# Two-layer block on one core: order of the heads, of the prologue and of the norms between layers changed

## The chip, the cores and the metric

One Trainium2 chip, one of its cores. The kernel is one launch on that core. The metric is the device time of an execution in microseconds (us); three executions of the kernel before stand below. Engines are named as the profile names them: PE is TensorE, DVE VectorE, ACT ScalarE, POOL GpSimd, SP SyncE.

## The reference

A sequence of 512 tokens with 1024 features (and a context of 256 tokens) goes through a block of two layers and then through one hybrid layer. What matters here:

```python
# layer 0 (even mixer)
hx = modulate(rmsnorm(x, g0), shift, scale)      # shift, scale, gate = silu(c) @ mod_w[0] + mod_b[0]
hc = modulate(rmsnorm(ctx, g0), shift_c, scale_c)
# 8 heads of 128 features, first over the context (for the state), then over x
u  = depthwise_conv(xb, sconv_w, sconv_b)        # 4 taps
r, i = sigmoid(u @ w_r + b_r), sigmoid(u @ w_i + b_i)
a  = exp(-8 * r * softplus(-lam));  bx = sqrt(1 - a*a) * i * u
h[t] = a[t] * h[t-1] + bx[t]                     # one scan forward, one backward
y_b = (h_forward + h_backward) * silu(gb)
y_a = silu(layernorm(conv31(va * sigmoid(vg)))) * silu(ga)
x = x + gate * (concat(y_a, y_b) @ w_out)
# layer 1 (odd mixer)
x = x + gate1 * pooled_mixer(modulate(rmsnorm(x, g1), shift1, scale1))
x = rmsnorm(x, final_g)
# hybrid layer: h = rmsnorm(x, norm1_g), four branches, merge, feed-forward, last rmsnorm
```

The output is (1, 512, 1024) in float32.

## The kernel before

Activations lie with features on the 128 partitions and tokens along the row: a tile is 128 features by 512 tokens (256 for the context), and X, h_hi, h_lo have 8 of them. A float32 product is made of three passes: weights and activations are each split into a high and a low part (float32r), and `three` multiplies high by high, high by low and low by high. `blocks` does this for up to 8 blocks of 128 features; a whole product of 24 matmuls of 512 columns is one "chunk" of weights.

Weights come in 284 chunks of 512 KB in the order of `NAMES`. Each goes through a ring of four slots: SP issues its DMA (L382), ACT makes the high part (`hi`, L412), DVE the low part (`lo`, L843), each three chunks ahead of the product (`ahead`). PE waits for the low part (`ready`). All engines run a fixed program in order; the order of the work of an engine is the order of the code in `act()`, `dve()`, `pe()`, and semaphores tie them.

**Prologue.** ACT issues the DMAs of the modulation weights (`mod0`, four of 2 MB), of X (2 MB) and of the context (1 MB). PE forms the modulation rows (`mod_rows`, L1466, two columns of weights and 128 moving columns at a time) and turns them into columns (`mod_columns`, L1472). ACT squares the tiles of X, DVE adds the squares up (L884), one matmul with ones sums over the features and spreads the sum over all partitions (`feature_sum`, L1459), ACT takes the root and DVE the reciprocal (L888). Then `norm_low` and `norm_high` (L912, L434, L919) make the 8 tiles of the context and then the 8 of X. After the last of them POOL issues the DMA of c for the other modulation columns (`csb`, L393), and ACT waits for it before the first head (L476).

**Heads.** First eight heads over the context (products xc, vg, va, gc), then eight over x (xb, gb, ga, gx, and the convolution cw of 31 taps, 128x32 tiles of the array, L1541). In each, ACT copies xb into `xp` (L485), DVE does the four taps (L977, L980), ACT and DVE split u (L489, L852), PE multiplies by the gates (gc or gx), ACT evaluates the gates (`head_gates`, L499 to L506), DVE forms the drive (`head_drive`, L990, L991), ACT takes two roots (`head_roots`, L511), DVE scans (`head_scan`, L997 to L1005), and in the heads over x adds, multiplies and splits the result (L1048, L1051, L552, L852). All of one head is done before ACT and DVE go on to the next one's xb. DVE also does 32 reductions of 128x1024 (`conditioning`, L904), two in each head, whose operand POOL loads two ahead (`MOD_RING`).

**After the heads.** PE sums csum, DVE subtracts the mean from the 8 tiles of U (mu, L1065, L1069), ACT squares them, DVE adds, PE sums, and meanwhile PE does the products yb 0 to 2, then yb 3 to 7 and ya 0 to 7. **Between layers** (after ya, and after od) DVE adds the product to X, ACT squares, DVE adds the squares, PE sums over features (128x512), ACT takes the root and DVE the reciprocal of 128x512; then norm tile by tile, and the first product (u 0, or qk 0) takes the tiles as they come. Between layer 1 and the hybrid layer there are two such sums, and X is scaled by the second afterwards.

Of the kernel before, what the change touches and what calls it, by code (L numbers as in the profile page):

```python
# [13 lines left out]
AHEAD = 3  # L14
KC = 8
# [23 lines left out]
def vector_columns():  # L39
    at, cols = 0, {}  # L40
    for name, n in (
# [5 lines left out]
        ("ssm_d", 2), ("ssm_norm_g", 2), ("norm2_g", NT), ("final_g2", NT), ("w_dt", NT * NH),  # L47
# [48 lines left out]
def bank_uses():  # L96
# [27 lines left out]
    "vec x ctx cst cst2 out hi lo mm crep csb mdv v a zero eps pad sil sp_z sp_e wdt rows cols rows_c x_sum x_sq fsum f_sq "  # L124
    "norm_t norm_hi norm_lo xp conv uhi ulo gread e2 mv sq thr scan sig uu "
    "tgt sgb sgat sga cpe csum yact ybhi yblo ymu usum usq yln ysil yga yhi yalo res xsq xsum "
    "lpad lcp dhi dsub dlo gsil gy gyhi gylo ores osq osum hsum "
    "bk4 bk5 bk6 bk7 ya_hi ya_lo yb_hi yb_lo yc_hi yc_lo yd_hi yd_lo ctap cact dtm dts dte dta "
    "st_qk st_abs st_ln st_sp st_in st_zb st_w st_wp st_pv mo_qk mo_mx mo_p mo_n mo_pt mo_cp mo_pv "
    "ma_cs ma_xt ma_xd ma_gm ma_gc ma_tri ma_abc ma_row ma_d ma_e ma_dk ma_pv ma_yt ma_sq ma_y mp mt mhi mlo "  # L130
    "wres wg whi wsq wsum wlo fg fsil fup fr fhi flo fres fsq fss fin"
# [40 lines left out]
def program(nc, wts, modw, modt, crep, vecs, consts, x_in, ctx_in, out):  # L172
# [66 lines left out]
    yb_hi = p("yb_hi", NT * T, F32R)  # L239
    yb_lo = p("yb_lo", NT * T, F32R)  # L240
    mraw = p("mraw", MOD_RING * CW)
# [16 lines left out]
    sq, rstd0, rstd_c, ssum = (aa[0], aa[1]), th[0], th[1], tg  # L258
# [4 lines left out]
    csil = small[:, 0:2 * NT]  # L263
# [12 lines left out]
    cs3 = csil.rearrange("p (k two) -> p k two", two=2)  # L276
    mv0 = modv0.rearrange("p (k two) -> p k two", two=2)
# [4 lines left out]
    rstd_b = at("rstd_b", T, limit // 32 * 32 - 2 * K * 5)  # L282

# [9 lines left out]
    rstd1, n_t1 = lev0[0][:, 0:T], [lev[:, T * k:T * (k + 1)] for k in range(3)]  # L293
# [26 lines left out]
    rstd2, r2, n_t2 = zs[:, 0:T], zs[:, T:2 * T], [bc[:, T * k:T * (k + 1)] for k in range(3)]  # L320
# [37 lines left out]

    def sp():
# [13 lines left out]
        e.wait_ge(s_mod0[1], 16)  # L373
        for c in range(N_CHUNKS):
# [13 lines left out]
    def pool():  # L388
# [9 lines left out]
        e.wait_ge(S["osum"], 2 * (NT - 1))  # L398
        e.dma_start(cst2[:, :], consts[:, 512:NCONST]).then_inc(S["cst2"], 16)

    def act():
# [25 lines left out]

        def norm_high(q, w, hi_t, shift, tmps):
# [8 lines left out]
        for j in range(4):  # L437
            e.dma_start(mod0[:, j * 4 * CW:(j + 1) * 4 * CW].rearrange("p (a n) -> p a n", a=4),
                        modw[4 * j:4 * j + 4, :, :].rearrange("a p n -> p a n")).then_inc(s_mod0[j], 16)
            if j == 0:  # L440
                e.dma_start(X[:, :], x_in).then_inc(S["x"], 16)
            if j == 1:
                e.dma_start(ctx_x[:, :], ctx_in).then_inc(S["ctx"], 16)
# [9 lines left out]
        e.wait_ge(S["x"], 16)  # L453
        for k in range(NT):
            if k > 2:
                e.wait_ge(S["x_sum"], k - 2)
            fn(ssum[:, :] if k == 0 else sq[k % 2][:, :], tile(X, k), ACT.Square).then_inc(S["x_sq"], 1)
        e.wait_ge(S["eps"], 1)
        root(1, rstd0, 0, eps_rms, D)
        e.wait_ge(S["ctx"], 16)  # L460
        for k in range(NT):
            e.wait_ge(S["x_sum"], NT - 1 + max(k - 2, 0))
            fn(ssum[:, 0:TC] if k == 0 else sq[k % 2][:, 0:TC], tile(ctx_x, k, TC), ACT.Square).then_inc(S["x_sq"], 1)
        for j in range(2):
            e.wait_ge(S["rows"], j + 1)
            fn(rows0[0:2, j * T:(j + 1) * T], bank(2 + j)[0:2, :], ACT.Copy).then_inc(S["rows_c"], 1)
        root(2, rstd_c[:, 0:TC], 1, eps_rms, D, TC)
        for c in range(AHEAD):
            hi(c)
        for j in range(2, 4):  # L470
            e.wait_ge(S["rows"], j + 1)
            fn(rows0[0:2, j * T:(j + 1) * T], bank(2 + j)[0:2, :], ACT.Copy).then_inc(S["rows_c"], 1)
# [18 lines left out]
        def head_gates(I, w, gates):  # L491
            if I:
                e.wait_ge(S["scan"], I)
# [38 lines left out]
        for i in range(NT):  # L532
# [3 lines left out]
            if i:  # L536
                convolved(i - 1)
# [1431 lines left out]
```

## Time and profile before

| | |
|---|---|
| three executions | 1792.26 us median, 1791.04 to 1792.68 |
| the profiled execution's own time | 1792.62 us |
| its span, first to last instruction | 1791.3 us |
| mean granted TensorE clock | 0.970 |
| PE busy | 1673.2 us, 93% |
| DVE busy | 992.5 us, 55% |
| ACT busy | 746.1 us, 42% |
| POOL busy | 19.4 us |

The span leaves 1.3 us of the execution's time outside. Busy PE counts a matmul from its start to its modelled end; matmuls overlap, so one of 512 columns is some 0.39 us long while the next begins 0.23 us after it. The rest of the profile is read as waits: in a timeline row the bracket says how long the engine was idle before this row and what released it.

### The profile page before, as it was taken

To read this page: it belongs to the slowest core of one execution; us is meant where nothing else is said; L and a number is where in the kernel's file an instruction comes from. 1 tells how busy PE (TensorE), PEld (TensorE's weight loads), DVE (VectorE), ACT (ScalarE), POOL (GpSimd) and SP (SyncE) were. 2 spreads that over 40 slices of the span, in tenths; PEclk is the share of its full clock that TensorE was granted. 3 is DMA by queue.
4 is the path that set the end of the run, shared out by engine and by line. 5 is a ranking of instruction groups with operands and counts; after the bars stand their busy time and mean duration, and the time that the engine had idled before them with its cause. 6 is when DMAs were issued, how large, how long until landed. Compare 5 with 4: busy or idle time off the path is not lost.

```text
span 1791.3 us, 19102 instructions
## 1 busy us (share of the span) xinstructions
PE 1673.2 (93%) x7670; PEld 1297.0 (72%) x7670; DVE 992.5 (55%) x1362; ACT 746.1 (42%) x1014; POOL 19.4 (1%) x40
## 2 busy tenths in 40 slices
PE   6798899996997999999799989999999999999996
PEld 4677666664785888888587857776677788888885
DVE  4677768777757556744744453345545544444333
ACT  3567665765434333332334444334433322332221
POOL 0000000000000000000000000000000000000000
PEclk9799999998998999999899989999999999999998
DMA  7345536454231233232132111221122233232321
GB/s 315 117 159 182 190 129 202 150 178 154 71 106 59 94 97 104 91 100 94 46 111 69 67 47 55 77 70 56 62 94 95 83 102 98 95 94 94 106 94 47
DMA packets 55063, 190.46 MB, mean 106 GB/s; under 512 B 7328, under 2 KB 7328, under 8 KB 54720
## 3 DMA queue, kind: packets, MB, share of 16 engines
q1 hardware_dynamic: 47616, 159.52, 27.4%
q0 software_dynamic: 4960, 18.20, 3.1%
q10 hardware_dynamic: 2400, 11.53, 1.6%
q8 instruction: 61, 1.00, 0.2%
q14 instruction: 26, 0.21, 0.0%
HBM read 178.63 MB, written 2.10 MB: 101 GB/s over the span
## 4 chain that ended last, share of the span: by engine, by line
PE 71%; DVE 14%; ACT 10%; issue 4%; ACTq 1%; DMA 0%; DVEq 0%
PE banks L1446 21%; PE banks L1448 21%; PE banks L1447 21%; ACT w_hi L412 2%; PE banks L1693 2%; DVE w_lo L843 2%; DVE u L980 2%; PE banks L1466 1%; ACT aa L504 1%; ACT tr L506 1%; DVE ti L997 1%; DVE tr L1001 1%; DVE tr L1005 1%; ACT tr L499 1%; PE banks L1715 1%
## 5 line engine op out<-in xcount | busy, mean ns | idle before, releaser
L1446 PE MATMUL banks<-h_hi,w_hi 128*128 128x512 f32 x1408 | 561.1, 398 | 24.4 <-DVE h_lo L919 10.3
L1447 PE MATMUL banks<-h_lo,w_hi 128*128 128x512 f32 x1408 | 553.1, 393 | 0.0
L1448 PE MATMUL banks<-h_hi,w_lo 128*128 128x512 f32 x1408 | 552.3, 392 | 0.0
L843 DVE TENSOR_TENSOR w_lo<-raw,w_hi 128x1024 fp32r<-128x1024 f32 x276 | 336.5, 1223 | 295.5 <-ACT w_hi L412 295.1
L412 ACT ACTIVATE w_hi<-raw 128x1024 fp32r<-128x1024 f32 x276 | 288.2, 1050 | 159.2 <-PE banks L1448 147.8
L1446 PEld LDWEIGHTS banks<-h_hi,w_hi 128*128 128x128 f32 x1408 | 266.7, 189 | 102.6 <-issue 34.4
L1448 PEld LDWEIGHTS banks<-h_hi,w_lo 128*128 128x128 f32 x1408 | 267.3, 190 | 56.9
L1447 PEld LDWEIGHTS banks<-h_lo,w_hi 128*128 128x128 f32 x1408 | 267.5, 190 | 53.8 <-issue 0.7
L1446 PE MATMUL banks<-y_hi,w_hi 128*128 128x512 f32 x192 | 76.8, 400 | 5.7 <-ACT gs L716 5.6
L1448 PE MATMUL banks<-y_hi,w_lo 128*128 128x512 f32 x192 | 76.8, 400 | 0.0
L1447 PE MATMUL banks<-y_lo,w_hi 128*128 128x512 f32 x192 | 76.1, 396 | 0.0
L1448 PE MATMUL banks<-f_hi,w_lo 128*128 128x512 f32 x176 | 70.2, 399 | 0.0
L1447 PE MATMUL banks<-f_lo,w_hi 128*128 128x512 f32 x176 | 69.4, 394 | 0.0
L1446 PE MATMUL banks<-f_hi,w_hi 128*128 128x512 f32 x176 | 69.0, 392 | 0.0
L716 ACT ACTIVATE gs<-banks 128x512 f32<-128x512 f32 x32 | 19.1, 598 | 110.9 <-PE banks L1448 110.8
L1541 PE MATMUL banks<-rep,raw 128*32 128x512 f32 x512 | 56.8, 594 | 0.0
L1446 PEld LDWEIGHTS banks<-y_hi,w_hi 128*128 128x128 f32 x192 | 36.4, 190 | 16.7 <-issue 4.4
L1414 DVE TENSOR_TENSOR fs<-banks,fs 128x512 f32<-128x512 f32 x22 | 15.2, 692 | 55.7 <-PE banks L1448 55.7
L1466 PE MATMUL banks<-mod,small 128*2 128x128 f32 x256 | 32.5, 295 | 13.9 <-ACT small L447 13.9
L1124 DVE TENSOR_TENSOR lev<-lev 128x632 f32<-128x632 f32 (+3 forms) x40 | 31.6, 791 | 24.5 <-ACT lev L598 23.5
L823 ACT ACTIVATE f_hi<-fs 128x512 fp32r<-128x512 f32 x22 | 13.9, 633 | 73.0 <-DVE fs L1416 73.0
L1447 PEld LDWEIGHTS banks<-y_lo,w_hi 128*128 128x128 f32 x192 | 36.4, 190 | 8.9
(347 smaller groups left out, 2145.8 us busy)
## 6 DMA issues: line engine op xcount, KB each, us to landing
raw<-weights SPq DMA_DIRECT2D x284, 512.0 KB, 3.5
mraw<-modt POOLq DMA_DIRECT2D x32, 512.0 KB, 4.5
mod<-modw ACTq DMA_DIRECT2D x4, 2048.0 KB, 23.0
rep<-U SPq DMA_DIRECT2D x96, 64.9 KB, 2.7
rep<-U SPq DMA_DIRECT2D x32, 64.8 KB, 2.5
X<-x_in ACTq DMA_DIRECT2D x1, 2048.0 KB, 13.2
out<-X SPq DMA_DIRECT2D x4, 512.0 KB, 2.7
ctx_x<-ctx_in ACTq DMA_DIRECT2D x1, 1024.0 KB, 19.8
```

Of the source, the lines that this page charges most:

```text
L412: fn(slot(w_hi, c), slot(raw, c), ACT.Copy).then_inc(S["hi"], 1)
L499: own.did(fn(tr[k][:, 0:w], gates[2 * k], ACT.Tanh, bias=at_c(144), scale=0.5))
L716: fn(gs[j][:, :], bank(4 + j), ACT.Sigmoid).then_inc(free("mg", br, half, j), 1)
L843: tt(slot(w_lo, c), slot(raw, c), slot(w_hi, c).bitcast(F32), ALU.subtract).then_inc(S["lo"], 1)
L980: m = stt(u[:, 0:w], xp[:, k:k + w], sw(k), u[:, 0:w], ALU.mult, ALU.add)
L1124: own.did(tt(here[:, :, wn // 2:wn // 2 + n], below[:, :, shift0:shift0 + n], below[:, :, shift0 + wn // 2:shift0 + wn // 2 + n], ALU.add))
L1446: mm(o, wh, r_hi, start=start, stop=False)
L1447: mm(o, wh, r_lo, start=False, stop=False)
L1448: return mm(o, wl, r_hi, start=False, stop=stop)
L1466: last = mm(bank(2 + j)[0:2, t * P:(t + 1) * P], csil[:, 2 * k:2 * k + 2], w, start=k == 0, stop=k == KC - 1)
L1541: last = mm(banks[32 * j:32 * j + 32, 3 * 512:4 * 512], slot(raw, c, (8 * j + step) * 32, 32), rep[i % 2][:, a:a + T], start=step == 0, st ...
L1693: last = mm(banks[p0:p0 + HD, OUT * 512 + n * P:(OUT + 1) * 512], v[:, n * 256 + h * HD:n * 256 + (h + 1) * HD], blk(w, n), start=n == 0, ...
```

## The change

Six things are changed.

1. Prologue: ACT issues X in two halves, the context, then the modulation weights in another layout (128 rows of 16 KB each) in the order of groups 0, 2, 1, 3, with the first three chunks of weights between the second and third group. `mod_rows` takes 32 stationary columns and 512 moving ones in four column groups of the array; `mod_columns` is a product with `pick`. The squares are summed by eight matmuls with ones instead of DVE adds. The norm's tiles come in two halves of the features: context 0 to 3, x 0 to 3, then context 4 to 7, x 4 to 7, and the first products (xc, vg, va of head 0) likewise, with `mod_rows(3)` and `mod_columns(2)`, `(3)` among them.
2. Heads as a pipeline of two: the roots, the drive, the scans and the result of head i-1 are done during head i. `conditioning` is done once in a head over the context and three times in a head over x. In heads over x the result lies in tr[0] instead of u; one of the tensors th has eight buffers.
3. After the heads, the first seven eighths of yb 0, 1, 2 come before the last head's result is needed; csum is summed after the first of them.
4. Norm between layers by columns of tokens: `token_sum` multiplies the squares (stationary, 128x128) by a column, so that sums lie with tokens on partitions (128x4); root and reciprocal are of 128x4; `token_scales` makes four diagonal blocks and `spread` multiplies ones by them, and the norm reads the result from PSUM. The sum of the first seven tiles is begun inside the last product.
5. The first two products after each of these norms go together, tile by tile.
6. The three memsets before the pooling are moved from DVE to POOL; X is scaled by the final norm behind products qk 0 to 2, and PE waits for that (`xfin`) ahead of the attention.

```diff
@@ sp, pool
-        e.wait_ge(s_mod0[1], 16)
-        for c in range(N_CHUNKS):
+        e.wait_ge(s_mod0[2], 16)
+        for c in range(AHEAD, N_CHUNKS):
...
+        e.wait_ge(S["norm_lo"], 3 * NT)
+        for t in (lev0[0], lev0[1], lev):
+            e.memset(t[:, :], 0.0).then_inc(S["lpad"], 1)
@@ act
-        for j in range(4):
-            e.dma_start(mod0[:, j * 4 * CW:(j + 1) * 4 * CW].rearrange("p (a n) -> p a n", a=4),
-                        modw[4 * j:4 * j + 4, :, :].rearrange("a p n -> p a n")).then_inc(s_mod0[j], 16)
...
+        for j in range(2):
+            e.dma_start(X[:, j * 4 * T:(j + 1) * 4 * T], x_in[:, j * 4 * T:(j + 1) * 4 * T]).then_inc(S["x1" if j else "x"], 16)
+        e.dma_start(ctx_x[:, :], ctx_in).then_inc(S["ctx"], 16)
+        for j, g in enumerate(GROUPS):
+            if j == 2:
+                for c in range(AHEAD):
+                    e.dma_start(slot(raw, c), wts[c, :, :]).then_inc(s_raw[c], 16)
+            e.dma_start(mod0[:, j * 4 * CW:(j + 1) * 4 * CW], modr[g, :, :]).then_inc(s_mod0[j], 16)
...
+        rows_copy(0)
+        rows_copy(1)
         for c in range(AHEAD):
             hi(c)
+        for n in range(4):
+            first_high(n)
+        rows_copy(2)
+        for n in range(4, 7):
+            first_high(n)
+        rows_copy(3)
+        first_high(7)
...
@@ act, heads over the context and over x
             head_input(i, TC, 4)
+            head_high(i, TC)
             ahead("vg", i)
+            if i:
+                head_roots(i - 1)
...
-            head_roots(i, TC)
...
             ahead("xb", i)
+            if i:
+                convolved(i - 1)
+            head_roots(NT + i - 1)
             product("xb", i)
             head_input(NT + i, T, 0)
             if i:
-                convolved(i - 1)
+                head_high_out(i - 1)
+            head_high(NT + i, T)
...
-            head_roots(NT + i, T)
-            e.wait_ge(S["yact"], i + 1)
-            fn(tile(yb_hi, i), u[:, :], ACT.Copy).then_inc(S["ybhi"], 1)
         convolved(NT - 1)
+        head_roots(2 * NT - 1)
+        head_high_out(NT - 1)
@@ dve, heads over the context
             ahead("xc", i)
-            head_input(i, TC)
+            if i:
+                head_drive(i - 1, TC)
+            head_conv(i, TC)
             ahead("vg", i)
+            head_low(i, TC)
+            if i:
+                context_scan(i - 1)
             ahead("va", i)
+            conditioning(i)
...
@@ dve, heads over x
             ahead("xb", i)
-            head_input(NT + i, T)
+            head_drive(NT + i - 1, T if i else TC)
             if i:
                 convolved(i - 1)
+                head_sum(i - 1)
+            else:
+                context_scan(NT - 1)
+            head_conv(NT + i, T)
+            if i:
+                head_low_out(i - 1)
             ahead("gb", i)
+            head_low(NT + i, T)
+            conditioning(NT + 3 * i)
...
@@ dve, between layers
-        inverse(4, rstd1)
-        norm_low(2, X, T, rstd1, lambda k: g1[:, k:k + 1], lambda k: modv1[:, k:k + 1], h_hi, h_lo, n_t1)
+        token_scales(4, 0)
+        e.wait_ge(S["rb"], 1)
+        norm_low(2, X, T, bank(6), lambda k: g1[:, k:k + 1], lambda k: modv1[:, k:k + 1], h_hi, h_lo, n_t1)
+        def token_scales(n, o):
+            e.wait_ge(S["f_sq"], n)
+            own.did(e.reciprocal(rc[:, o:o + NB], rc[:, o:o + NB]))
+            own.wait()
+            for j in range(NB):
+                ts(dg[:, j * P:(j + 1) * P], ident, rc[:, o + j:o + j + 1], None, ALU.mult).then_inc(S["dg"], 1)
@@ pe
+        def token_sum(b, total, w, start, stop):
+            n = w.shape[1]
+            for j in range(NB):
+                last = mm(bank(b, n, n * j), total[:, j * P:(j + 1) * P], w,
+                          start=start and j == 0, stop=stop and j == NB - 1)
+            return last
+        def spread(b, n):
+            for j in range(NB):
+                e.wait_ge(S["dg"], NB * n + j + 1)
+                last = mm(bank(b, P, j * P), ones, dg[:, j * P:(j + 1) * P], start=True, stop=True)
+            last.then_inc(S["rb"], 1)
         def mod_rows(j):
             e.wait_ge(s_mod0[j], 16)
-            for t in range(4):
-                for k in range(KC):
-                    w = mod0[:, (4 * j + t) * CW + k * P:(4 * j + t) * CW + (k + 1) * P]
-                    last = mm(bank(2 + j)[0:2, t * P:(t + 1) * P], csil[:, 2 * k:2 * k + 2], w, start=k == 0, stop=k == KC - 1)
+            for k in range(KC):
+                q = k % 4
+                last = mm(bank(ROWS_BANK[j])[32 * q:32 * q + 32, :], cs[:, 32 * k:32 * k + 32],
+                          mod0[:, j * 4 * CW + k * T:j * 4 * CW + (k + 1) * T], start=k < 4, stop=k > 3)
...
         for f in range(3):
-            yb(f)
+            yb_early(f)
+            if f == 0:
+                e.wait_ge(S["csum"], NT)
+                feature_sum(0, csum[:, :])
+        for f in range(3):
+            yb_late(f)
         e.wait_ge(S["usum"], NT - 1)
         feature_sum(1, ti[0][:, :])
...
+                blocks(bank(BANK_OF[f]), c, h_hi, h_lo, n=5, start=False, stop=False)
+                e.wait_ge(S["xsum"], NT - 2)
+                token_sum(7, s1[:, :], s_one, True, False)
+                blocks(bank(BANK_OF[f]), c, h_hi, h_lo, b0=5, k0=5, n=3, start=False).then_inc(S["mm"], 1)
...
+            if g == 0:
+                c0, c1 = ready("u", 0, 0), ready("u", 0, 1)
+                for k in range(KC):
+                    e.wait_ge(S["norm_lo"], 2 * NT + k + 1)
+                    m0 = three(bank(0), c0, k, tile(h_hi, k), tile(h_lo, k), k == 0, k == KC - 1)
+                    m1 = three(bank(1), c1, k, tile(h_hi, k), tile(h_lo, k), k == 0, k == KC - 1)
```

## Rows read from the trace of the kernel before

**Rows 1.** The page's first part: busy time, share of span, instructions of each engine.

```profile
PE 1673.2 (93%) x7670; PEld 1297.0 (72%) x7670; DVE 992.5 (55%) x1362; ACT 746.1 (42%) x1014; POOL 19.4 (1%) x40
```

**Rows 2.** Timeline of the prologue: start, length, engine, line, operation; idle before and releaser.

```profile
3.02 9.14 ACTq L438 DMA_DIRECT2D mod<-modw  x2
...
41.81 8.81 PE L1466 MATMUL banks<-mod,small 128*2 128x128 f32 x64
...
52.32 0.88 DVE L912 SCALAR_TENSOR_TENSOR n_t<-ctx_x,small,th 128x256 f32<-128x256 f32 x2
...
68.81 1.63 DVE L919 SCALAR_TENSOR_TENSOR h_lo<-n_t,small,h_hi 128x512 fp32r<-128x512 f32 x2
...
74.74 1.06 ACT L476 ACTIVATE csb<-csb 128x1024 f32<-128x1024 f32 x1 [3.78 <-DMA csb<-crep]
```

**Rows 3.** Windows: length, busy time of each engine, PE clock, DMA share, GB/s.

```profile
20.00:36.00 16.00, 16.00 (x141) 11.78 (x139) 6.59 (x7) 6.04 (x10) 0.00 (x0) 1.00 1.02 408
```

**Rows 4.** Timeline of ACT and DVE in one head over the context.

```profile
121.54 0.47 ACT L499 ACTIVATE tr<-banks,small 128x256 f32<-128x256 f32 x1
...
126.06 0.42 DVE L990 SCALAR_TENSOR_TENSOR th<-tr,th 128x256 f32<-128x256 f32 x1 [1.44 <-ACT tr L506]
...
127.98 1.05 ACT L412 ACTIVATE w_hi<-raw 128x1024 fp32r<-128x1024 f32 x1
...
131.46 1.21 DVE L843 TENSOR_TENSOR w_lo<-raw,w_hi 128x1024 fp32r<-128x1024 f32 x1
...
134.59 0.42 ACT L489 ACTIVATE u_hi<-u 128x256 fp32r<-128x256 f32 x1 [5.30 <-DVE u L980]
...
139.66 0.46 ACT L499 ACTIVATE tr<-banks,small 128x256 f32<-128x256 f32 x1
```

**Rows 5.** Timeline of ACT, DVE and PE in one head over x.

```profile
400.52 0.69 ACT L499 ACTIVATE tr<-banks,small 128x512 f32<-128x512 f32 x1
...
410.68 0.69 DVE L997 TENSOR_TENSOR ti<-ti,xp 128x512 f32<-128x512 f32 x1
...
416.36 0.63 ACT L552 ACTIVATE yb_hi<-u 128x512 fp32r<-128x512 f32 x1 [5.78 <-DVE u L1051]
...
418.56 0.47 PE L1446 MATMUL banks<-h_hi,w_hi 128*128 128x512 f32 x1 [0.81 <-ACT xp L485]
...
422.85 0.63 ACT L489 ACTIVATE u_hi<-u 128x512 fp32r<-128x512 f32 x1 [4.43 <-DVE u L980]
...
427.27 7.09 PE L1541 MATMUL banks<-rep,raw 128*32 128x512 f32 x64
...
428.24 0.69 ACT L499 ACTIVATE tr<-banks,small 128x512 f32<-128x512 f32 x1
```

**Rows 6.** All uses of the modulation columns' operand: time from issue to landing.

```profile
DMA to landing us min/median/max: 3.7/4.5/7.8
```

**Rows 7.** Timeline of PE and DVE after the last head.

```profile
447.22 2.08 PE L1459 MATMUL banks<-csum,cst 128*128 128x512 f32 x2 [12.87 <-DVE csum L1029]
...
449.34 0.69 DVE L1065 TENSOR_SCALAR aa<-banks 128x512 f32<-128x512 f32 x1 [1.80 <-PE banks L1459]
...
468.04 1.12 PE L1459 MATMUL banks<-ti,cst 128*128 128x512 f32 x2 [0.49 <-DVE ti L1076]
```

**Rows 8.** Windows after that idle time, columns as in rows 3.

```profile
448.00:452.00 4.00, 4.00 (x9) 2.68 (x8) 1.98 (x3) 1.21 (x3) 0.00 (x0) 0.50 0.00 0
```

**Rows 9.** Timeline between layers 0 and 1.

```profile
540.88 0.75 DVE L1094 SCALAR_TENSOR_TENSOR X<-banks,small,X 128x512 f32<-128x512 f32 x1 [1.81 <-PE banks L1448]
...
550.78 0.77 PE L1446 MATMUL banks<-h_hi,w_hi 128*128 128x512 f32 x1 [6.58 <-DVE h_lo L919]
...
558.64 0.50 PE L1446 MATMUL banks<-h_hi,w_hi 128*128 128x512 f32 x1 [0.36 <-DVE h_lo L919]
```

**Rows 10.** Line 1761: matmuls with a stationary 128x128 float32 operand, ns.

```profile
L1761 PE MATMUL banks<-av,cst x20: 167/252/253, 1189.1 to 1191.1; 128*128 128x4 f32 x20
```

**Rows 11.** Timeline between layer 1 and the hybrid layer: the first product.

```profile
874.83 0.76 PE L1446 MATMUL banks<-h_hi,w_hi 128*128 128x512 f32 x1 [5.16 <-DVE h_lo L852]
```

More of the change, by code:

```diff
@@ L275, in program @@
     cb2, gn, nsp8 = small[:, 354:362], small[:, 362:370], small[:, 370:386]
-    cs3 = csil.rearrange("p (k two) -> p k two", two=2)
-    mv0 = modv0.rearrange("p (k two) -> p k two", two=2)
+    cs3 = cs.rearrange("p (k m) -> p k m", m=32)
+    pick = cols("pick", 2)
+    mv0 = modv0.rearrange("p (a k two) -> p a k two", a=3, two=2)
+    first = [(q, k) for half in range(2) for q in range(2) for k in range(4 * half, 4 * half + 4)]
+    place = {qk: n for n, qk in enumerate(first)}
     u3 = U[:, :].rearrange("p (f w) -> p f w", w=UW)
@@ L464, in act @@
[L464 to L467 removed]
+        for n in range(2 * NT):
+            if n % 4 == 0 and n < NT:
+                e.wait_ge(S["x1" if n else "x"], 16)
+            if n == NT:
+                e.wait_ge(S["ctx"], 16)
+            if n > 9:
+                e.wait_ge(S["x_sum"], n - 3)
+            elif n > 2:
+                e.wait_ge(S["x_sum"], min(n - 2, NT - 1))
+            if n == 10:
+                e.wait_ge(S["fsum"], 1)
+            src, w = (tile(X, n), T) if n < NT else (tile(ctx_x, n - NT, TC), TC)
+            fn(sq[n % 3][:, 0:w], src, ACT.Square).then_inc(S["x_sq"], 1)
+            if n == NT - 1:
+                e.wait_ge(S["eps"], 1)
+                root(1, rstd0, 0, eps_rms, D)
@@ L475, in act @@
+        rows_copy(3)
+        first_high(7)
+        for n in range(8, 16):
+            first_high(n)
         e.wait_ge(S["crep"], 16)
@@ L926, in dve @@
         own.did(e.memset(eps_ln, 4e-5))
+        own.did(e.memset(small[:, 388:389], EPS))
+        own.did(e.memset(small[:, 389:391], 1.0))
+        own.did(e.memset(cs, 0.0))
+        own.wait()
         e.memset(eps_sq, EPS * EPS).then_inc(S["eps"], 1)
@@ L1016, in dve @@
             ahead("gc", i)
-            head_drive(i, TC)
-            conditioning(2 * i)
-            head_scan(i, TC, lambda k: 0.0)
-            conditioning(2 * i + 1)
-            e.wait_ge(S["scan"], i + 1)
-            for k in range(2):
-                own.did(e.tensor_copy(ctx_state[:, 2 * i + k:2 * i + k + 1], tr[k][:, (TC - 1, 0)[k]:(TC, 1)[k]]))
         def convolved(i):
@@ L1378, in dve @@
         e.wait_ge(S["cst2"], 16)
-        run(inputs_qkv(0))
+        ahead("qk", 0, 0)
+        token_scales(6, NB)
+        ahead("qk", 0, 1)
+        ahead("qk", 0, 2)
+        e.wait_ge(S["rb"], 3)
+        for k in range(NT):
+            m = stt(tile(X, k), tile(X, k), col("final_g", k), bank(2), ALU.mult, ALU.mult)
+            if k < NT - 1:
+                own.did(m)
+            if k == 3:
+                ahead("qk", 0, 3)
+        m.then_inc(S["xfin"], 1)
+        e.wait_ge(S["xfin"], 1)
+        ahead("v", 0, 0)
+        ahead("v", 0, 1)
         products = strand(inputs_a(), inputs_qkv(1), inputs_c())
@@ L1796, in pe @@
         e.wait_ge(S["cst2"], 16)
+        c0, c1 = ready("qk", 0, 0), ready("qk", 0, 1)
+        b0, b1 = free("qk", 0, 0), free("qk", 0, 1)
+        for k in range(KC):
+            e.wait_ge(S["norm_lo"], 3 * NT + k + 1)
+            m0 = three(b0, c0, k, tile(h_hi, k), tile(h_lo, k), k == 0, k == KC - 1)
+            m1 = three(b1, c1, k, tile(h_hi, k), tile(h_lo, k), k == 0, k == KC - 1)
+        m0.then_inc(S["mm"], 1)
+        m1.then_inc(S["mm"], 1)
         run(inputs_qkv(0))
+        e.wait_ge(S["xfin"], 1)
         products = strand(inputs_a(), inputs_qkv(1), inputs_c())
```

391 lines of the change are left out of this document (220 added, 171 removed).

## Prediction

> **What bounds the kernel now.** I read the page first, then the windows, then the timeline stage by stage. PE is busy 93% of the span [rows 1], so only the other 7% and the slow matmuls inside the 93% can be won by reordering; the products themselves stay (284 chunks, some 5.46 us each: 24 matmuls, 0.2275 us apart). The chain of waits shows where PE stands still, and the change touches all of these places but none behind the first products of the hybrid layer:
>
> - Prologue: the norm's tiles begin at 52.32 and end at 70.44 [rows 2]. PE does modulation rows in 8.8 us a group. After the last tile ACT waits 3.8 us for c's DMA and silu runs at 74.74.
> - Heads over the context: gates start at 121.54 and again at 139.66, a period of 18.12 us [rows 4], eight times. PE's work in it is 2.84 + 2 x 5.46 + 1.4 = 15.2 us.
> - Heads over x: 400.52 to 428.24, 27.7 us [rows 5]. PE's work is 3 x 5.46 + 2.9 + 7.1 us and some 0.3 of switching, 26.7 us; 0.8 us is a wait for xp.
> - After the heads: 12.9 us of idle PE before csum's sum, and then nine matmuls in 4 us with the granted clock at 0.50, the 1.2 GHz level [rows 7, 8].
> - Between the layers: last product ended 540.8, first product at 550.78, its matmuls then paced by tiles 1.33 us apart [rows 9]; the same to 874.83 [rows 11].
>
> **The change part by part.** Signs: minus is faster.
>
> *Prologue.* X, the context and two groups are 7.3 MB, all of it with c's vectors and three chunks 13.5 MB. At the 408 GB/s of [rows 3] the last group lands near 35 us; before, that was no bound, as PE did its last group until 50.6 [rows 2]. If ACT is through its issues at some 6 us, squares start near 10.6. Eight sums of 512 float32 columns take PE 8 x 0.87 = 7 us (half a sum's matmul pair of [rows 7]'s 1.1 us is 0.43 to 0.56), to 18; root 2; the context's sums to 24. A modulation group is now 8 wide matmuls in four column groups; the convolution's 32 of this kind take 7.09 us [rows 5], so 1.8 us a group, or 3.6 with the clock at its lower level. Two groups to 27.6, columns 29.4. DVE has the three low parts in front of the gains, so the tiles start at 33 instead of 52.3. Half of the tiles take half of 18.1 us, so the first half is through at 42 to 43. The last two groups' rows and columns end at 45.7 (clock high) to 47.7 (low); the second half needs 0.6 + 9.1 us: last tile at 55.5 to 57.5. I take 56.6, 13.8 us earlier than 70.4. From there c's DMA, silu and xp follow as before. But in the first head DVE now does a low part before `head_low`, and ACT the matching high part: its gates start 1.9 us later behind silu. Net -11.9. The page "DMA: Bandwidth & Descriptors" of the Trainium skill (section Specifications) gives some 358 GB/s of HBM for a core; the trace disagrees, 408 GB/s for 16 us [rows 3]. By the page the last group would land near 40 us and the sum be some 2 us worse.
>
> *Heads over the context.* ACT's program is the loop. New order behind the gates: 4.5 us of gates (121.54 to 126.06), one high part (1.05), then DVE's low part and four taps (131.46 to 134.59, 3.1), before them the drive (four operations of 0.42 [rows 4], 0.34 apart, 1.4). That is the tap's end at 10.05. Then 134.59 to 139.66, 5.07, is u_hi to the next gates as before, and the roots with their table load, 1.93 (126.05 to 127.98), now lie within it. Sum 17.1 us for 18.12. What left the loop is the scan and one reduction. PE (15.2) is no bound, nor DVE (12.7 of work). Seven periods: -6.8. Bounds: 0 if another wait of the in-order programs closes the loop at 18.1; -20 if it fell to PE's 15.2.
>
> *Turn to x.* The reduction now stands ahead of uu, for which xb waits: PE starts xb 1 us later against the gates, the first gates of x come 0.8 earlier. I take -0.5 in all.
>
> *Heads over x.* ACT and DVE: gates 6.5 and two high parts to 8.5, low part's remainder 1.4, drive 2.45, csum 0.7, first multiplication to result 5.7 (410.68 to 416.36), taps 2.9, u_hi to the next gates 5.4 less the convolution's copy, which now lies elsewhere, 0.6 [rows 5]: 26.4 us. PE's own 26.7 is then the bound. 27.7 - 26.7 is 1.0, seven periods: -6.7. DVE has three reductions here, 22.2 us of work in 26.7. The third needs a slot whose DMA was issued a few us before (ring of two); landing takes 4.5 us, 7.8 at most [rows 6], and by the order above up to 8.2 us costs nothing.
>
> *After the heads.* PE now has 14.3 us of early yb to do, which fills the 12.9. But the second sum stays where DVE's chain puts it: mu to second sum was 18.7 us (449.34 to 468.04) [rows 7], and mu cannot start before the last head's result. Behind the last gates mu comes at 19.4 us instead of 21.1, so the second sum is 1.7 us earlier. In front of it PE has nothing left (yb 0 to 2 are done by 24.7 us, the sum starts at 38.1): 13.4 us of idle moved behind yb. And this idle is followed by the slow matmuls of [rows 8] in a place that bounds: nine at 0.43 instead of 0.23, first one 1 us late, the sum 1 us longer, some 3 us, less 0.4 that the wait there cost before. Net +0.9. This edit returns almost nothing of the gap it aims at.
>
> *Layer 0 to 1.* The path was: addition, square, addition of squares, sum, root, reciprocal of 128x512 (3.4 us), tile. Now the sum is 8 weight loads and matmuls, some 0.11 us apart as in [rows 10] (20 in 2.1 us), 0.85 us; root and reciprocal of 4 columns 0.2 each; four 128x128 products on DVE and the last spread, about 1.3 us, an estimate from the 0.42 us of 256 columns [rows 4]. First tile for PE at 548.1, with the 0.85 us of the inserted `token_sum` in it. The two products go together: 48 matmuls, eight at 0.43 while the clock is still low, 40 at 0.2275, end 561.1. Before, the second product ended at 560.2 + 5.46 = 565.6. -4.5. The memsets (3.7 us on DVE) move to POOL; the trace shows no large POOL memset. Below nothing they cannot be; they are needed for the high part of chunk u 2, which PE asks for 9 us after the last tile, so up to twice DVE's time is hidden. Upper end: three times, +3.
>
> *Layer 1 to 2.* Likewise, with two inserted sums (1.7 us on PE): first product at 872.6, both ended at 885.4 for 889.3. `spread(2, 2)` adds 1.05. -2.9. Scaling X is hidden by 17 us of v products.
>
> Sum: -11.9 - 6.8 - 0.5 - 6.7 + 0.9 - 4.5 - 2.9 = -32.4 us. From 1792.6 of the profiled execution that is 1760.2; this execution lies 0.4 above the median of three, so 1760 against 1792.3.
>
> **The rivals.**
>
> - *A, ACT's queue stays blocked.* The last two issues took 9.14 us, until 12.16 [rows 2], with some 7 MB not yet moved. If what filled the queue is bytes and not descriptors, ten DMAs of 12.5 MB hold ACT until 14 to 17 us and the squares with it. The rows are four times longer now, so fewer descriptors for the same bytes, which speaks against it. Prologue -3 instead of -12: 1769. Chance 0.15.
> - *B, the heads gain nothing.* Both loops are in-order programs with little slack (1 us). A wait that I didn't see on ACT or DVE closes them at the old length: 1773. Chance 0.15.
> - *C, more than forecast.* The context's heads fall towards 15.5 us, or the clock stays high in the gaps: 1744. For it: PE has work there; against: ACT's sum of 17.1. Chance 0.12.
> - *D, slower.* The third reduction in a head over x waits for its operand. Its DMA shares the engines with 16 replicas and a chunk. Each us above 8.2 costs 8 us; above 12.3 us the kernel is slower than before, at 13 us it takes 1798. Against it: the 7.8 us maximum of 32 [rows 6]. Chance 0.04.
> - *E, no change*, everything given back by idle time that only moves as after the heads, 1792. Against it: the norm's tiles and the 3.4 us reciprocal lie plainly on the path. Chance 0.04.
>
> A rule of the Trainium skill stands near C: "TensorE: Matmul & The Clock Gate", section on HAM oscillation, says that idle gaps lower the clock and dense work restores it. The trace agrees where the gap was long (0.50 after 12.9 us [rows 8]). It speaks against part 3, where the gap stays; that is in my sum from the row.
>
> **How the numbers follow.** Forecast 0.50, with its own range 1752 to 1768. A, B and C are taken in and D and E left out: 1744 to 1776. A difference of 0.2% (3.6 us) is about what a measurement of this kernel can tell from none. Faster: 0.50 + 0.15 + 0.15 + 0.12 = 0.92; same 0.03; slower 0.05 with D and part of E.
>
> **What would show it.** Last `h_lo` tile near 57 and silu near 61; squares from 10 to 11 (A: 17 or later). Period of context gates 17.1 (B: 18.1). Period over x 26.7, PE without the 0.8 us wait. PE idle some 13 us before the second sum after the heads, with clock 0.5 behind it. PE's first product between layers 7.3 us after the last one ended, u 0 and u 1 ending together 13 us after it began. Wrong would make it: ACT's issues, a slow POOL memset, a reduction that waits for its DMA.

## The result, and the profile after

The changed kernel takes 1798.53 us (median of 8 runs, 1795.1 to 1799.78) where the kernel before took 1792.36 (8 runs, 1790.53 to 1795.15): a ratio of 1.0029, 95% interval 1.0019 to 1.0039. The forecast was 1760. So it is slower by 6 us, and the forecast was off by 38.

The page's first part, after:

```profile
PE 1674.5 (93%) x7588; PEld 1299.4 (72%) x7588; DVE 971.5 (54%) x1360; ACT 747.2 (42%) x1014; POOL 23.1 (1%) x43
```

It looks like that of before [rows 1]: the page does not show where the time went. A table by stage does. Each row is the distance between two events that both traces have (start of ACT's first gate `tr<-banks`, ends of groups of PE's matmuls), before and after:

| stage | before | after | difference | forecast |
|---|---|---|---|---|
| start to the first gates | 83.88 | 75.73 | -8.2 | -11.9 |
| seven periods over the context | 128.25 | 120.97 | -7.3 | -6.8 |
| turn: last gates of the context to first of x | 22.13 | 23.75 | +1.6 | -0.5 |
| **seven periods over x** | 193.98 | 219.53 | **+25.6** | -6.7 |
| last gates to the end of ya | 112.60 | 114.08 | +1.5 | +0.9 |
| end of ya to the end of u and g, level 0 | 57.73 | 52.87 | -4.9 | -4.5 |
| from there to the end of the last qk | 301.87 | 302.50 | +0.6 | -2.9 |
| the rest | 890.86 | 888.47 | -2.4 | 0 |

The sum is +6.6, as the spans (1791.3 and 1797.9), where the forecast's parts add up to -32.4. One row explains 32.3 us of these 39.0: the heads over x follow each other at 30.9 to 32.2 us, 31.4 on average, not at 26.7. Windows over the heads over x, kernel before and then the changed kernel; columns: stretch, length, busy time of PE, its weight loads, DVE, ACT and POOL, granted clock, DMA share, GB/s:

```profile
230.00:434.00 204.00, 199.01 (x1119) 127.77 (x1117) 149.15 (x194) 129.40 (x179) 7.41 (x14) 1.00 0.51 163
```

```profile
230.00:446.00 216.00, 194.67 (x1022) 129.19 (x1024) 151.12 (x202) 122.92 (x167) 10.06 (x19) 0.94 0.52 165
```

PE stands still for 21 us in place of 5, and the granted clock falls to 0.94, that is, part of this stretch ran at the lower level, 1.2 GHz. For PE the view of waits over that stretch names only "issue", which tells nothing. Its row for ACT tells more: 26.9 us in seven waits for a load of weights; over the heads of the kernel before it has no such row (engine, line, what it waited for; us in total, times, longest):

```profile
PE banks L1547 <- issue: 21.3, 7, 3.2
ACT w_hi L434 <- DMA raw<-weights: 26.9, 7, 4.1
```

The timeline of the changed kernel for one head over x (ACT, DVE, PE and SP's queue; it answers to [rows 5]) tells it:

```profile
377.56 0.69 ACT L549 ACTIVATE tr<-banks,small 128x512 f32<-128x512 f32 x1 [1.12 <-PE banks L1549]
...
384.09 1.07 ACT L434 ACTIVATE w_hi<-raw 128x1024 fp32r<-128x1024 f32 x1
384.62 0.33 SPq L401 DMA_DIRECT2D raw<-weights  x1
388.88 1.06 ACT L434 ACTIVATE w_hi<-raw 128x1024 fp32r<-128x1024 f32 x1 [3.72 <-DMA raw<-weights]
...
391.11 0.69 DVE L1070 SCALAR_TENSOR_TENSOR thf<-tr,thf 128x512 f32<-128x512 f32 x1
...
402.62 0.63 ACT L537 ACTIVATE u_hi<-u 128x512 fp32r<-128x512 f32 x1 [2.19 <-DVE u L1058]
404.08 0.47 PE L1547 MATMUL banks<-u_hi,w_hi 128*128 128x512 f32 x1 [2.97 <-issue]
...
404.92 0.63 PE L1547 MATMUL banks<-u_hi,w_hi 128*128 128x512 f32 x1
...
408.70 0.69 ACT L549 ACTIVATE tr<-banks,small 128x512 f32<-128x512 f32 x1 [1.16 <-PE banks L1549]
```

ACT is through with the gates and a high part at 385.16. The next instruction of its program is the high part of chunk gx (`ahead("xb", i)` at the front of the loop). It waits 3.72 us for its load, which SP issued only at 384.62. The ring of raw chunks has four slots, so chunk gx of this head takes the slot of chunk cw of the head before, four places earlier; that one is not split, PE reads it itself, and starts its next product only at 384.48 (the modelled end of the convolution's last matmul is 384.55). Issue at 384.62, landing 4.2 us later. Behind the waiting instruction stand, in ACT's order, the convolution's copy, the roots, xp, the high part of y and u_hi, and in DVE's order, behind the low part of the same chunk, the whole recurrence. u_hi comes so late that PE has nothing to do for 3 us in front of gx; then most matmuls of gx follow each other at 0.43 us in place of 0.23 (granted clock 0.66 from 404 to 409 us), and the next gates wait for them. In the kernel before the same high part stood in the same place of the loop's text, but the roots and the recurrence were in front of it, not behind it, and by then, 16.4 us behind the first gates instead of 7.6, the chunk had long landed. The view of all uses of `raw` counts these waits too, in the changed kernel:

```profile
  DMA raw<-weights: 26.9, 7
```

Seven waits, 26.9 us. In the kernel before that view has no such line at all.

The Trainium skill has a rule for this: "DMA: Bandwidth & Descriptors", section "Anatomy of one DMA — SWDGE (gpsimd) path", says that the DMA engines themselves do not wait for semaphores; the sequencer that issues does, before dispatch. By that rule this load cannot be under way before SP's wait for the slot is over, and the trace agrees: it was issued 0.07 us behind the modelled end of the product that freed the slot.

### The profile page after: what moved, and what is told of

It is laid out like the page before. It is cut to its first block, busy times and chain, and to the rows that moved or that the text cites. A ratio compares the mean times of both kernels' runs of the same rounds, so it can differ in the third digit from the quotient of the medians.

```text
span 1797.9 us, 18924 instructions
## 1 busy us (share of the span) xinstructions
PE 1674.5 (93%) x7588; PEld 1299.4 (72%) x7588; DVE 971.5 (54%) x1360; ACT 747.2 (42%) x1014; POOL 23.1 (1%) x43
## 4 chain that ended last, share of the span: by engine, by line
PE 84%; DVE 6%; ACT 6%; issue 3%; ACTq 0%; DMA 0%; DVEq 0%
PE banks L1547 25%; PE banks L1549 24%; PE banks L1548 24%; PE banks L1678 3%; ACT w_hi L434 2%; PE banks L1870 2%; DVE w_lo L904 1%; PE banks L1597 1%; PE banks L1892 1%; PE banks L1960 1%; DVE u L1058 1%; PE banks L1914 1%; PE banks L1822 0%; ACT aa L554 0%; PE banks L1824 0%
## 5 line engine op out<-in xcount | busy, mean ns | idle before, releaser
L1549 PEld LDWEIGHTS banks<-h_hi,w_lo 128*128 128x128 f32 x1408 | 266.6, 189 | 56.6
L1548 PE MATMUL banks<-f_lo,w_hi 128*128 128x512 f32 x176 | 69.4, 394 | 0.0
L1547 PE MATMUL banks<-u_hi,w_hi 128*128 128x256 f32 (+1 forms) x64 | 28.2, 441 | 38.5 <-issue 21.3
L1547 PEld LDWEIGHTS banks<-u_hi,w_hi 128*128 128x128 f32 x64 | 15.1, 236 | 46.3 <-issue 24.1
```

The source lines that it names most:

```text
L1547: mm(o, wh, r_hi, start=start, stop=False)
L1548: mm(o, wh, r_lo, start=False, stop=False)
L1549: return mm(o, wl, r_hi, start=False, stop=stop)
```

## The experiments

All comparisons are with the kernel before, run on the same chip; its medians there were 1792.26, 1792.06, 1792.27 and 1791.43 us. A gain against the changed kernel, or against another experiment, is the difference of two medians, often from two chips; where the single executions of the two overlap, a difference of 1 or 2 us shows nothing by itself.

**1. The high part of gx later.** In ACT's loop over x (DVE's likewise, its low part behind `head_low`):

```diff
-            ahead("xb", i)
             if i:
                 convolved(i - 1)
...
             head_high(NT + i, T)
-            ahead("gb", i)
+            ahead("xb", i)
```

(`ahead("gb", i)` stood for a chunk cw, which is not split, and did nothing.)

> In the loop of the heads over x the high part of chunk gx, on ACT, moves from the front of the head to behind head_high, and its low part on DVE to behind head_low; nothing else changes. Theory T (the head over x is 31.1 us long because ACT's high part of gx stands first in its program and waits for a DMA that SP can issue only when the convolution of the head before is through, so that everything behind it in ACT's order comes 3.9 us late): the period of the gates falls from 31.1 to about 27 (26.7 is PE's work), the last convolution ends 28 to 35 us earlier, the kernel takes 1764 to 1771. Rival D (the third conditioning reduction waits for its operand): nothing changes by more than 3 us. Rival S (ACT's and DVE's own work of a head, summed in their orders, makes 30 us whatever the DMA does): less than 10 us gained, 1789 or more.

Measured: 1762.65 us, ratio 0.984 (0.9824 to 0.9857), 35.9 us faster than the changed kernel. The periods are 26.25 to 26.71. The window over the heads over x:

```profile
225.00:409.00 184.00, 184.00 (x1033) 122.19 (x1031) 151.54 (x203) 123.48 (x168) 10.06 (x19) 1.00 0.63 195
```

PE is busy for all of it, at the full clock. Theory T holds, S and D fall. But this moves an instruction as well as a wait; experiment 3 parts the two.

**2. The conditioning as before.** The forecast had named another load for this stage: the third reduction's operand (rival D). Two reductions in each head, as before the change:

```diff
-            conditioning(i)
+            conditioning(2 * i)
+            conditioning(2 * i + 1)
```

and over x two in place of three.

> The conditioning reductions stand as before the change: two in each head over the context and two in each head over x, in place of one and three. Theory T: the heads over x stay at 31.1 us, the context's at 17.1 or up to 0.3 more; 1796 to 1801. Rival D: the heads over x fall by 1.2 us (one reduction's length) or more each, 1789 or less.

Measured: 1798.59 us, ratio 1.0034 (1.0021 to 1.0046); periods over x 30.9 to 32.2, over the context 17.07. D falls: the right kind of cause on the wrong load. In the changed kernel's trace the loads for the reductions land within 5.6 us, and DVE has no row of waits for them.

**3. A slot of its own for the convolution's chunk.** ACT and DVE keep the changed kernel's order; the load alone comes early:

```diff
-                if WHOLE[c - RING]:
+                if WHOLE[c]:
                     e.wait_ge(S["mm"], c - RING + 1)
-                else:
+                elif not WHOLE[c - RING]:
                     e.wait_ge(S["lo"], N_SPLIT[c - RING] + 1)
...
+            dst = slot(raw_lo, c) if WHOLE[c] else slot(raw, c)
...
```

`raw_lo` is a second name for w_lo's bytes: a chunk of the convolution is not split, so its slot of w_lo is free. The lines cut here give it a semaphore of its own and let PE read it there.

> The changed kernel with ACT's and DVE's programs untouched. Only the raw chunk of the convolution is loaded into the slot of w_lo that it leaves unused, with a semaphore of its own, so that SP may issue chunk gx's load without waiting for the convolution of the head before. Theory T (ACT's first instruction of a head waits for a load that was issued too late): ACT's wait for raw in front of gx's high part, 3.7 us in every head, goes, the period over x falls from 31.1 to 27.3 or to PE's 26.7, the kernel takes 1765 to 1771, nearly as good as with the late gx. Rival O (the late gx helped because of another order of ACT's and DVE's work, and not because of the load): 1790 or more.

Measured: 1761.19 us, ratio 0.9835 (0.982 to 0.9849). ACT in one head of it, then its line in the view of the uses of `raw`:

```profile
348.29 0.69 ACT L552 ACTIVATE tr<-banks,small 128x512 f32<-128x512 f32 x1
...
354.82 2.01 ACT L437 ACTIVATE w_hi<-raw 128x1024 fp32r<-128x1024 f32 x2
356.72 0.68 ACT L585 ACTIVATE U<-banks,small 128x512 f32<-128x512 f32 x1
...
369.70 0.63 ACT L540 ACTIVATE u_hi<-u 128x512 fp32r<-128x512 f32 x1 [2.19 <-DVE u L1061]
...
374.69 0.69 ACT L552 ACTIVATE tr<-banks,small 128x512 f32<-128x512 f32 x1
```

```profile
  DMA raw<-weights: 0.2, 1
```

The two high parts now follow each other, as the forecast had assumed, and the period is 26.40. Same order on ACT and DVE, no late load, same gain: the cause is the load.

**4. The output product not begun early.** csum's sum, then yb 0 to 2 whole:

```diff
-            yb_early(f)
...
-            yb_late(f)
+            yb(f)
```

> The output product after the heads is not begun with seven heads' tiles: csum's sum, then yb 0 to 2 whole, as before the change; all else stays. Step of the prediction (this edit only moves 13 us of idle from in front of csum's sum to in front of the second sum, and puts the slow matmuls into a place that bounds, some 3 us for it): 1 to 3 us faster than the changed kernel, 1795 to 1798. Rival (the early products gain): 3 us or more slower, 1802 or more.

Measured: 1795.03 us, ratio 1.0016 (1.0007 to 1.0026), 3.5 us faster than with the edit. From the end of the last convolution to the end of ya 104.5 us, against 107.1 with it (106.9 to 107.3 in experiments 1 to 3): 2.6 of the 3.5 lie there. In the changed kernel, PE's second sum (it answers to [rows 7]) and the window behind it, columns as above:

```profile
477.78 2.08 PE L1560 MATMUL banks<-ti,cst 128*128 128x512 f32 x2 [12.83 <-DVE ti L1170]
```

```profile
478.00:482.00 4.00, 4.00 (x8) 2.48 (x9) 1.39 (x1) 2.09 (x3) 0.00 (x0) 0.50 0.28 112
```

The 12.87 us of idle PE that stood in front of csum's sum [rows 7] is 12.83 in front of the second one, and the slow matmuls come with it. The 120 matmuls behind are 255 ns apart, 238 before.

**5. Two more products in front of the second sum**, on top of 1: `for f in range(3, 5): yb(f)` ahead of its wait.

> The kernel with the late gx (1762.65), in which PE does yb 3 and yb 4 before the second sum after the heads and not behind it. Their chunks are converted by 426 and 432 us of the profile, their products fit into the 12.8 us of idle PE. The second sum comes at its old time or at most 1 us later, PE stays at its high clock, three yb are left behind the sum; the first ya then waits for the norm's tiles, the last of which is ready at 472 us, so that some 8 us of the gained 13 come back as that wait: 2 to 5 us faster, 1757.5 to 1760.5. Rival (the end of the stage is set by PE's work alone): 11 to 13 us faster, 1750. Rival (the tiles set it): no gain.

Measured: 1760.64 us, ratio 0.983 (0.9813 to 0.9846), 2.0 us faster than experiment 1. The single executions of the two overlap (1760.53 to 1763.2 and 1761.01 to 1765.85); the gain rests on the stage, 104.6 us from the last convolution to the end of ya, where experiments 1 to 3 have 106.9 to 107.3. The idle in front of the sum fell to 1.6 us, but the first ya, with less work ahead of it, waits for the tiles of y, 6.5 us in five waits, this one the longest:

```profile
465.19 0.79 PE L1545 MATMUL banks<-h_hi,w_hi 128*128 128x512 f32 x1 [3.17 <-DVE h_lo L912]
```

**6. DVE's conversions one step later**, on top of 5. DVE's low part of a weight chunk waited for ACT's high part 1.65 us four times and 1.05 us three times:

```diff
-            if k % 3 == 1:
+            if k % 3 == 2:
                 ahead("yb", k // 3)
```

and in the loop over the tiles of y from the head of a step to its end.

> The kernel with yb 3 and yb 4 in front of the second sum (1760.64), in which DVE's low parts of the weights after the heads stand one step later in its program, so that it does not wait for ACT's high part (1.65 us three times before the second sum, 1.06 us five times in the norm's tiles). The second sum comes at 29 us behind the last convolution in place of 30.8, PE being done with yb 4 by then; the last tile of y comes 6 to 9 us earlier and the 5 us of waits in the first ya go: 4 to 6 us faster, 1754.6 to 1756.6. Rival (ACT's order sets the pace of the tiles): 0 to 2 us.

Measured: 1754.66 us, ratio 0.9788 (0.9774 to 0.9803), 6.0 us faster. From the last convolution to the end of ya 95.3 us, for 104.6 in experiment 5 and 106.9 in experiment 1. PE no longer stands still before the second sum:

```profile
441.50 1.02 PE L1558 MATMUL banks<-ti,cst 128*128 128x512 f32 x2
```

So the gap behind the heads was worth 11.6 us of the stage in all with the filling and the shorter chain of DVE together (8.0 in the medians; in this profile the first gates came 1.6 us later than in experiment 1, and the turn to x took 1.3 longer); filling alone gave 2. The shorter chain without the filling was not run, so how the rest divides between the two stays open.

**7. Three edits of the prologue**, each on top of 1. First the second half's columns right behind their rows:

```diff
                         mod_rows(3)
-                    elif name == "vg":
                         mod_columns(2)
```

> The kernel with the late gx (1762.65), in which PE makes the second half's modulation columns right behind their rows, before the first half of vg. The gains of the second half's tiles come 2.5 to 3 us earlier, and with them the last tile, silu and the first gates: 2 to 3 us faster, 1759.7 to 1760.7. Rival (PE's products of the first half set the end): no change or 1 us slower.

Measured: 1760.87 us, ratio 0.983 (0.9816 to 0.9845), 1.8 us faster than experiment 1. This is no gain shown: the single executions overlap (1760.63 to 1764.01 and 1761.01 to 1765.85), and the first gates came at 72.02 us, where the same prologue without the edit gave 72.17 to 72.81 in four profiles.

Then c's load issued in front of POOL's wait:

```diff
+        e.dma_start(csb[:, :], crep).then_inc(S["crep"], 16)
         e.wait_ge(S["norm_lo"], 2 * NT)
-        e.dma_start(csb[:, :], crep).then_inc(S["crep"], 16)
```

> The kernel with the late gx (1762.65), in which POOL issues the load of c (0.5 MB) before it waits for the last tile of the prologue and not behind that wait. ACT's wait of 3.5 us in front of silu goes; the load shares the first 35 us with 13.5 MB and may delay the modulation's groups by 1 us. 2 to 3.5 us faster, 1759 to 1760.7. Rival (the first gates are bound by PE, which ends the last product of the prologue after silu): less than 1 us.

Measured: 1763.15 us, ratio 0.9838 (0.9823 to 0.9852), 0.5 us slower. ACT's wait is gone, yet silu begins at 61.58, as in experiment 1 (61.59), since the last tile comes 3.5 us later. This run alone does not settle why: its sums over the context ended 2.5 us later than those of experiment 1 (28.4 and 25.9 us), and among the profiles of experiments 1 to 6 and of the changed kernel that time already differs by 2.8 (25.4 to 28.2).

Last, ten products of zeros in front of PE's first sum, work that the output does not need:

```diff
+        for _ in range(10):
+            mm(bank(7), U[:, 0:P], U[:, 0:T], start=True, stop=True)
```

> The kernel with the late gx (1762.65), in front of whose first sum PE multiplies a tile of zeros 10 times, into a bank that is started anew later; DVE sets that tile to zero first. It adds work that the output doesn't need. Theory (the sums of the prologue and the modulation rows run at the lower of PE's two clock levels, because PE stood still until 10.3 us; how long they do differs from run to run and makes the 3.7 us between the profiles' first gates, 72.0 to 76.2): the eight sums over X are paced by ACT's squares, the context's sums end near 24 us, the first gates come at 70 to 71.5, 2 to 3 us faster than the kernel with the late gx: 1759.5 to 1761. Rival (the clock has no part in it, loads have): no change.

Measured: 1764.02 us, ratio 0.9837 (0.9817 to 0.9856), no faster. The products ended at 13.0 us, 2.6 us after the first square was ready, and put the sums off. The expectation was wrong.

**8. All together**, with ten products of zeros, none, and six. These three kernels have one edit more that was never run by itself: the first two products of ya go together, tile by tile, as those between the layers do.

> All edits together: late gx, yb 3 and yb 4 before the second sum, DVE's conversions later, the two first products of ya together by tiles, columns early, c loaded early, PE kept busy before its first sum. If they add up: late gx 1762.65, less 2 for yb 3 and yb 4, 5 for the conversions, 1 to 2 for the two ya together, 1.8 for the columns, 2.5 for the busy PE and up to 3 for c: 1747 to 1751. If the prologue's three share one gain, 1751 to 1754.

> All edits together (1747.97) without the ten products of zeros in front of PE's first sum. If those products only cost (they ended at 11.7 and 13.0 us in the two runs that had them, 1.3 to 2.6 us after the first square was ready): 0 to 2 us faster, 1746 to 1748. If the clock that they raise is worth more: 1 to 3 us slower, 1749 to 1751.

> All edits together, with six products of zeros in place of ten, so that they end near 8 us, ahead of the first square at 10.4. Theory (PE at the higher level of its clock from the first sum on is worth 2 us, and ten products were too many): 1 to 3 us faster than without them. Rival (PE stands still for 2.4 us again between the products and the sums and behind the sums over X, and the sums over the context start at the lower level anyway): within 1 us of the kernel without them.

Measured: 1747.97 us with ten, ratio 0.9754 (0.9739 to 0.9768); 1747.54 with none, 0.9757 (0.9743 to 0.9771); 1746.11 with six, 0.9745 (0.9731 to 0.976). Ten products show no gain. Six may: all five executions with them (1744.65 to 1747.23) lie below all five without (1747.37 to 1748.38), taken together on one chip, 1.4 us apart in the medians. But the first gates of the two profiles are only 0.4 us apart (65.82 and 66.23), so that the zeros save it by the clock in the prologue, as expected, is not shown. With c and the columns early together the first gates come at 65.8 to 69.4 us, for 72.0 with the columns alone; silu, which waited 3.83 us for c there, waits no more in any of the three. So c's early load does pay beside them. The best version is 45 us faster than the kernel before on the same chip, and 52 faster than the changed one.

## Why the prediction was wrong, point by point

- **Heads over x: wrong, -6.7 forecast, +25.6 measured.** The step that failed is the first term of the sum for ACT and DVE, "gates 6.5 and two high parts to 8.5". It took the second high part to follow the first. It didn't ask where its operand comes from: in the kernel before the instruction never waited, so the trace had no row for it, and the moved instruction brought the wait along. The prediction did ask this of the conditioning reductions, the loads that the diff moves visibly, and not of the instruction that stayed in its line of the loop while everything around it moved. In the head shown the gates and the two high parts end 12.4 us behind the first gate, not 8.5. Against the head of experiment 3 (8.5 there) that brings u_hi 3.65 us later; another 1.1 us come between u_hi and the next gates, where the matmuls of gx are slow behind the idle time. Together that is the 4.7 between 31.1 and 26.4. With the wait gone (experiments 1 and 3) the period is 26.4 to 26.5, the forecast 26.7: PE has no idle time left, and the 0.3 us of switching that the forecast gave it did not show. The rest of that sum was right. Rival B had given a wait that wasn't seen a chance of 0.15, but let it only eat the gain of 6.7; it cost nearly five times that. Rival D gave the right time, 1798, for the wrong load: experiment 2 rules it out.
- **Heads over the context: right**, 17.07 for 17.1. (Seven times the 1.02 between 18.12 and 17.1 is 7.1, not the 6.8 of the sum; measured 7.3.) The same high part stands first there too, but all four chunks of such a head are split, so the slots come free early.
- **Prologue: mechanism right, size off.** ACT's issues were through at 6.2 us and the squares began at 9.50, so rival A falls. The term that was mis-sized is PE's sums over X and the context: they ended at 27.84 for a forecast 24, and all that follows is as much later (first tile 37.08 for 33, last tile 60.4 for 56.6, first gates 3.7 late). The first four records of these sums took 0.94 us each and the last ones over X 0.47, and the granted clock was 0.81 and 0.77 from 20 to 24 and 24 to 28 us. From silu on the forecast held (gates 11.2 us behind it, for 11.0). In the seven profiles whose prologue is the same (the changed kernel and experiments 1 to 6) the first gates came at 72.2 to 76.2 us, so this stage has 4 us of spread that no edit makes: in four of them the context's sums ended at 25.4 to 25.9 and the first gates came at 72.2 to 72.8, nearly the 72.0 of the forecast; in three they ended at 27.8 to 28.2, with the gates at 74.4 to 76.2. What decides between the two is not shown.
- **Turn to x: wrong by 2.1.** PE starts xb 2.2 us behind the last context gates for 1.1 before, as forecast. But from there to the first gates of x it took 0.5 us more than before (21.5 for 21.1), where the -0.5 in all needed a gain of 1.5; what held them is open.
- **After the heads: right in mechanism and nearly in size**, +1.5 for +0.9: "13.4 us of idle moved behind yb" was 12.8.
- **Layer 0 to 1: right**, -4.9 for -4.5, first product 7.24 us behind ya's end (7.3 forecast). The memsets took 3.70 us on POOL, as long as they had on DVE; the slow memset that the forecast feared did not come.
- **Layer 1 to 2: wrong by 3.5.** The mis-sized term is the two sums by columns of tokens behind the last product. They were put at 0.85 us each, by a row with a busy PE [rows 10]. The same 16 records took 1.84 us inside the last product, on a busy PE; here PE had just waited, and the granted clock was 0.60 from 875 to 879 us:

```profile
875.34 3.19 PE L1566 MATMUL banks<-small,s 128*128 128x2 f32 x16 [1.50 <-ACT s L699]
```

  That is 1.5 of the 3.5. The first `spread` behind them took 2.07 us, 0.75 more than the one after ya, and 12 starts of the first two products were some 0.43 us apart where the forecast had eight for such a pair, 0.8 more. From the end of od to the first product 9.97 us, for 11.12 before; the 1.84 us of the inserted sums and 1.05 of the late `spread` take more than that. No run undid this edit alone; this is read from the trace.
- **The rest, -2.4, is no effect of the change.** The same products run there; in the first 195 us of it the granted clock was 0.97, for 0.95 before. Profiles of two kernels with the same program in that part differ as much: from the first pooled product to the last sum 1177.8 us in the changed kernel, 1174.7 in experiment 4.

The range, 1744 to 1776, failed since none of the cases in it priced this load. Without the late load the changed kernel lies where it was forecast: 1761.19 and 1762.65 for 1760. Part of that closeness is luck: in the profile of experiment 3 the heads over x gave 2.6 us more than forecast and those over the context 0.6 more, and the turn (1.5), the stage after the heads (0.5), the prologue (0.4) and the rest (1.3) gave less.

## What to carry to other kernels

When a loop is turned into a pipeline, list for every instruction that now stands nearer to the front what it waits for, its load's slot included: who used that slot last, when does that use end, and how long before the instruction is the issue. An instruction that waits for nothing in the old trace has no row that warns of it. Where one chunk of a ring is held longer than the others, the chunk that follows it in its slot is the one to place last or to give another slot. And idle time in front of a sum that is filled may come back behind it, where the next product waits for the chain that the sum feeds: here filling gave 2 us, filling and shortening that chain 8.

## What the runs showed of the hardware

- Behind the idle time of 2.8 to 3.3 us in front of gx, in seven heads of eight, PE fell to its lower level: in the head shown, from the fourth matmul of gx on they took 0.63 us with starts 0.43 apart (the row at 404.92 above is the first). The granted clock was 0.66 from 404 to 409 us and 0.94 from 230 to 446 us, and it was 1.00 with the gap gone. So a gap of 2.97 us costs this head 4.6 of PE's time: gx took 4.5 us for 2.9. The Trainium skill ("TensorE: Matmul & The Clock Gate", section "HAM oscillation — how this bites in real kernels") says of a matmul kernel that idle gaps in which PE waits for a load put the next group of matmuls at the lower level, every time; the trace agrees for these seven gaps.
- At the start of a profile the granted clock and the durations disagree. Four matmul records at the beginning of the sums over X and four near their end, all in windows with a granted clock of 1.00:

```profile
10.26 3.75 PE L1597 MATMUL banks<-aa,cst 128*128 128x512 f32 x4 [10.26 <-ACT aa L493]
...
18.15 1.88 PE L1597 MATMUL banks<-aa,cst 128*128 128x512 f32 x4
```

  The same work takes twice the time at first, as between the two levels, while the column says 1.00 both times; that the durations are right and the column wrong is a reading, which no run here tests. Ten products of zeros from 1.46 us on took 11.56 us in one run and 10.28 in another.

- PE's own row of waits named only "issue" for its 21.3 us in seven gaps. The load stood in ACT's row of the same view and in the uses of the loaded tile (26.9 us, seven times): the cause of a bounding engine's idle time is looked for in the waits of the engines that feed it.
